# Hybrid decoder layer on eight cores: another arrangement of the last output tiles, and a later slot for the decode masks

## What is computed

```python
h = rmsnorm(x, norm_gain)
q, k, v, g_gla, gk_lr, u, b_gate, c_gate, g_conv = split(h @ w_in)
o, S_new = gla(q, k, v, log_sigmoid(gk_lr @ w_gk_up + b_gk) / 16, S0)   # gated linear attention, 4 heads
o = rmsnorm(o, gla_norm_gain) * silu(g_gla)
yc = b_gate * conv3(c_gate * u) * silu(g_conv)                           # 512 channels
out = x + concat(o, yc) @ w_out
y = rmsnorm(out, final_norm_gain)
```

## Time and profile before

| | |
|---|---|
| median of 3 runs | 315.29 us (314.78 to 315.7) |
| profiled execution | 317.33 us |
| its span on the slowest core (core 1), first to last instruction | 315.8 us |
| spans of the other cores | 311.4 to 314.9 us |
| PE busy | 294.1 us (93%) |
| DVE busy | 236.6 us (75%) |
| ACT busy | 183.9 us (58%) |
| POOL busy | 88.0 us (28%) |

### The profile page before, as it was taken

How to read it: one execution, slowest core, us unless ns; L and a number is a source line. 1 busy time by engine, 2 the same in 40 slices (tenths; PEclk the granted TensorE clock), 3 DMA queues, 4 the chain that set the end, 5 groups by cost and what they waited for, 6 DMA issues and landing times.

```text
span 315.8 us, 6265 instructions; the slowest of 8 cores (311.4 to 315.8 us)
## 1 busy us (share of the span) xinstructions
PE 294.1 (93%) x1870; PEld 147.5 (47%) x1870; DVE 236.6 (75%) x414; ACT 183.9 (58%) x490; POOL 88.0 (28%) x96
## 2 busy tenths in 40 slices
PE   0399999999999979999999999999999999999991
PEld 0284444455444645644444344545444445554460
DVE  3446674979867679999966597899974837889565
ACT  3618535694774538757536668786428536464245
POOL 2995000123233315222332332113306132101050
PEclk9999899999999999999999999989999999999996
DMA  6999999999125032376998743464573311102445
GB/s 162 204 165 163 166 163 170 290 177 202 67 52 185 30 108 95 94 179 144 194 220 243 241 118 113 159 196 35 135 181 136 101 66 66 36 17 66 130 166 208
DMA packets 39873, 44.57 MB, mean 141 GB/s; under 512 B 20952, under 2 KB 29920, under 8 KB 39456
## 3 DMA queue, kind: packets, MB, share of 16 engines
q1 hardware_dynamic: 34800, 32.06, 37.9%
q0 software_dynamic: 4752, 11.77, 21.7%
q10 hardware_dynamic: 288, 0.35, 0.3%
HBM read 38.16 MB, written 10.95 MB: 156 GB/s over the span
## 4 chain that ended last, share of the span: by engine, by line
PE 90%; issue 2%; DVE 2%; DMA 2%; ACT 2%; DVEq 0%; ACTq 0%
PE ps L673 45%; PE ps L683 17%; PE ps L886 8%; PE ps L841 7%; DMA idp_sb<-idp 2%; PE ps L649 2%; PE ps L669 2%; PE ps L1083 2%; PE ps L935 1%; PE ps L797 1%; PE ps L770 1%; PE ps L772 1%; DVE hT L651 1%; PE ps L1238 1%; PE ps L897 1%
## 5 line engine op out<-in xcount | busy, mean ns | idle before, releaser
L673 PE MATMUL ps<-hT,w_in_bf 128*128 128x512 bf16 x656 | 152.6, 385 | 0.2 <-DVE X L692 0.2
L673 PEld LDWEIGHTS ps<-hT,w_in_bf 128*128 128x128 bf16 x656 | 63.7, 99 | 73.3 <-issue 11.0
L703 POOL TENSOR_TENSOR X<-X,fg_sb 128x1024 f32<-128x1024 f32 x14 | 33.9, 2420 | 83.4 <-ACT xs L603 42.9
L660 ACT ACTIVATE f<-ps 128x512 f32<-128x512 f32 (+1 forms) x34 | 19.8, 585 | 39.8 <-PE ps L673 21.4
L603 ACT ACTIVATE xs<-X 128x1024 bf16<-128x1024 f32 x29 | 30.5, 1051 | 20.4 <-DVE X L692 17.5
L683 PE MATMUL ps<-w_out_bf,mixC 128*128 128x512 bf16 (+1 forms) x136 | 35.3, 367 | 0.0
L683 PE MATMUL ps<-w_out_bf,mixG 128*128 128x512 bf16 (+1 forms) x136 | 33.2, 367 | 0.0
L692 DVE TENSOR_TENSOR X<-ps,X 128x512 f32<-128x512 f32 x28 | 19.1, 687 | 18.4 <-PE ps L683 17.8
L886 PE MATMUL ps<-w_v_bf,hT 128*128 128x512 bf16 x128 | 29.5, 379 | 0.0
L841 PE MATMUL ps<-w_in_bf,hT 128*128 128x512 bf16 x96 | 22.7, 379 | 0.0
L661 ACT ACTIVATE f<-f 128x512 f32<-128x512 f32 (+1 forms) x34 | 20.9, 618 | 1.7
(11 more groups left out here) (196 smaller groups left out, 456.2 us busy)
## 6 DMA issues: line engine op xcount, KB each, us to landing
X<-x_all SPq DMA_DIRECT2D x23, 512.0 KB, 5.6
y<-X SPq DMA_DIRECT2D x14, 512.0 KB, 2.9
w_in_bf<-w_in_l POOLq DMA_DIRECT2D x24, 256.0 KB, 21.3
w_out_bf<-w_out_l POOLq DMA_DIRECT2D x2, 1024.0 KB, 51.1
X<-gla_in SPq DMA_DIRECT2D x8, 256.0 KB, 4.7
gla_s<-X SPq DMA_DIRECT2D x8, 256.0 KB, 4.5
w_v_bf<-w_v_l POOLq DMA_DIRECT2D x1, 1024.0 KB, 23.0
X<-x_all POOLq DMA_DIRECT2D x2, 512.0 KB, 37.6
```

Source lines behind the costliest of these rows:

```text
L660: op("act", lambda e: e.activation(out=f.t[:, 0:W], in_=bank.t[:, 0:W], func=AF.Exp, scale=-1.0), dur, [bank.r], [f.r], key, fill)
L673: op("pe", lambda e: [e.matmul(out=bank.t[:], lhsT=w_in_bf[:, c, kc, :], rhs=hT.t[:, kc, :], start=(kc == 0), stop=(kc == KC - 1)) for kc ...
L703: op("pool", lambda e: e.tensor_tensor(out=xb.t[:], in0=xb.t[:], in1=fgb.t[:], op=ALU.mult), 2.4, [xb.r, fgb.r], [xb.r], key + 2, fill)
```

## The change

Four edits:

1. Decode masks: each group's four masks are planned at a cost of 1.6 instead of 1.0 us, and not earlier than 14 planner microseconds before the group's key (112, 124, 136, 148). The instructions are the same.
2. Item 3, tile 1 (`whole`): gain and scaling in one VectorE instruction instead of GpSimd's L703 and a scaling.
3. Item 3, tile 2: Square by halves with a running sum, gain and scaling in two VectorE instructions of 512 columns, each with its store.
4. Item 3, tile 3: one half and two quarters in place of four quarters; the gain of the left half in one GpSimd instruction of 512 columns in place of two VectorE ones of 256. In item 3 the matmuls of the right half of tile 1, and all of tiles 2 and 3, are one operation of 8 instead of 7 and 1. The buffers of tiles 2 and 3 are tracked by half, and by half and quarters.

```diff
-        def out_tile(lhs, parts, m_res, rows, r0, key, fill=False, xb=None, port_free=False, lead=14):
+        def out_tile(lhs, parts, m_res, rows, r0, key, fill=False, xb=None, port_free=False, lead=14, whole=False):
...
+            def half_done(hf, bank):
+                cs = slice(hf * 512, (hf + 1) * 512)
+                op("dve", lambda e: e.tensor_tensor(out=xb.t[:, cs], in0=bank.t[:], in1=xb.t[:, cs], op=ALU.add), 0.69,
+                   [bank.r, xb.R[hf]], [xb.R[hf]], key + hf)
+                op("act", lambda e: e.activation(out=junk2.t[:, cs], in_=xb.t[:, cs], func=AF.Square, accum_out=sums.t[:, hf:hf + 1]), 0.77,
+                   [xb.R[hf]], [junk2.R[hf], sums.R[hf]], key + hf)
+                if hf == 0:
...
+                    return
...
+                for q in range(2):
+                    qs = slice(q * 512, (q + 1) * 512)
+                    op("dve", lambda e, qs=qs: e.scalar_tensor_tensor(out=xb.t[:, qs], in0=xb.t[:, qs], scalar=sums.t[:, 4:5], in1=fgb.t[:, qs],
+                                                                      op0=ALU.mult, op1=ALU.mult), 0.75, [xb.R[q], sums.R[4], fgb.r], [xb.R[q]], key + 2)
+                    dma("sp", lambda e, qs=qs: e.dma_start(out=y_d[r0:r0 + rows, qs], in_=xb.t[0:rows, qs]), _Slot(None, "yt2_%d" % q), [xb.R[q]], [],
+                        key + 3, rows * 2 * KB, out=True)
...
-            if port_free:
+            if whole:
                 op("dve", lambda e: e.scalar_tensor_tensor(out=xb.t[:], in0=xb.t[:], scalar=st.t[:, 2:3], in1=fgb.t[:], op0=ALU.mult, op1=ALU.mult),
                    1.28, [xb.r, st.r, fgb.r], [xb.r], key + 3)
...
         def out_tile_last(lhs, parts, m_res, r0, key, xb):
...
-            for q in range(4):
+            W = [slice(0, 512), slice(512, 1024)]
+            Q = [slice(0, 512), slice(512, 768), slice(768, 1024)]
+            for q in range(3):
                 bank = PS.new()
+                n = Q[q].stop - Q[q].start
+                out_mm(bank, slice(0, 512) if q == 0 else slice(q * 256 - 256, q * 256), 1 if q else 0, lhs, parts[1], m_res, key + 0.1 * q, False)
...
-                if q < 2:
-                    op("dve", lambda e, q=q: e.tensor_tensor(out=pf.t[:, Q[q]], in0=xb.t[:, Q[q]], in1=fgb.t[:, Q[q]], op=ALU.mult), 0.4,
-                       [xb.R[q], fgb.r], [pf.R[q]], key + 0.1 * q)
+                if q == 0:
+                    op("pool", lambda e: e.tensor_tensor(out=pf.t[:, W[0]], in0=xb.t[:, W[0]], in1=fgb.t[:, W[0]], op=ALU.mult),
+                       1.25, [xb.R[0], fgb.r], [pf.r], key)
...
+            if last and t:
+                parts = [parts if t == 1 else [(0, 8, [b.r for b in mc])], [(0, 8, [b.r for b in mc])]]
+            else:
+                parts = [parts, parts]
...
                 op("dve", lambda e, G=G, vmv=vmv: [e.tensor_scalar(out=vmv()[:, s, :], in0=vts.t[:],
                                                                    scalar1=prm_t[:, PO_SEL + 4 * G + s:PO_SEL + 4 * G + s + 1], scalar2=None,
-                                                                   op0=ALU.mult) for s in range(4)], 1.0, [vts.r, prm.r], [vm.r], kg, True)
+                                                                   op0=ALU.mult) for s in range(4)], 1.6, [vts.r, prm.r], [vm.r], kg, True, kg - 14.0)
```

More of the change, by code:

```diff
@@ L685, in out_mm @@
                 op("pe", mm, 0.163 + (hi - lo) * (n / 2400.0 + 0.0025), m_res + res + [B_wout[hf].r], [bank.r], key, fill)
-        def out_tile(lhs, parts, m_res, rows, r0, key, fill=False, xb=None, port_free=False, lead=14):
+        def out_tile(lhs, parts, m_res, rows, r0, key, fill=False, xb=None, port_free=False, lead=14, whole=False):
             xb = xb or x_load(r0, key - lead, key - lead)
+            if port_free:
+                sums = one("sums", [128, 5], F32, 5)
+                junk2 = XS.new(2)
+            def half_done(hf, bank):
[5 more added lines that the diff above has]
+                if hf == 0:
+                    op("act", lambda e: e.activation(out=sums.t[:, 2:3], in_=sums.t[:, 0:1], func=AF.Identity, scale=1.0 / D, bias=EPS),
+                       0.25, [sums.R[0]], [sums.R[2]], key)
+                    return
+                op("act", lambda e: e.activation(out=sums.t[:, 3:4], in_=sums.t[:, 1:2], func=AF.Ln, scale=1.0 / D, bias=sums.t[:, 2:3]), 0.25,
+                   [sums.R[1], sums.R[2]], [sums.R[3]], key + 1)
+                op("act", lambda e: e.activation(out=sums.t[:, 4:5], in_=sums.t[:, 3:4], func=AF.Exp, scale=-0.5), 0.2,
+                   [sums.R[3]], [sums.R[4]], key + 1)
+                for q in range(2):
[4 more added lines that the diff above has]
+                        key + 3, rows * 2 * KB, out=True)
@@ L733, in out_tile_last @@
[L733 to L744, removed]
+            junk = XS.new(3)
@@ new lines, in out_tile_last @@
+            op("act", lambda e: e.activation(out=acc.t[:, 5:6], in_=acc.t[:, 2:3], func=AF.Ln, scale=1.0 / D, bias=acc.t[:, 4:5]), 0.25,
+               [acc.R[2], acc.R[4]], [acc.R[5]], key + 1)
+            op("act", lambda e: e.activation(out=acc.t[:, 6:7], in_=acc.t[:, 5:6], func=AF.Exp, scale=-0.5), 0.2,
+               [acc.R[5]], [acc.R[6]], key + 1)
+            fo = [_Res(), _Res()]
+            op("act", lambda e: e.activation(out=xb.t[:, W[0]], in_=pf.t[:, W[0]], func=AF.Copy, scale=acc.t[:, 6:7]), 0.72,
+               [pf.r, acc.R[6], xb.R[0]], [fo[0]], key + 1)
@@ new lines, in out_tile_last @@
+            op("dve", lambda e: e.scalar_tensor_tensor(out=xb.t[:, W[1]], in0=xb.t[:, W[1]], scalar=acc.t[:, 6:7], in1=fgb.t[:, W[1]],
+                                                       op0=ALU.mult, op1=ALU.mult), 0.75, [acc.R[6], fgb.r] + xb.R, [fo[1]], key + 1)
+            for h, q in enumerate(("act", "sp")):
+                dma(q, lambda e, h=h: e.dma_start(out=y_d[r0:r0 + 128, W[h]], in_=xb.t[:, W[h]]),
+                    _Slot(xb, "yl%d" % h), [fo[h]], [], key + 1, 256 * KB, out=True)
@@ L1026, in item @@
                 hb = HT.new(5)
-                late = [_Part(hb, hb.R[0:1], 0, 1024), _Part(hb, hb.R[1:5], 1024, 2048)]
+                late = [_Part(hb, hb.R[0:2], 0, 1024), _Part(hb, hb.R[2:5], 1024, 2048)]
                 for k, xb in enumerate(late):
@@ L1038, in item @@
                     out_tile(lhs, parts, [m.r], 128, r0 + t * 128, base + 70 + 6 * t + (6 if i == 0 else 0),
-                             xb=kept[t] if i == 0 else late[0] if last and t == 2 else None, port_free=last and t > 1, lead=20 if last else 14)
+                             xb=kept[t] if i == 0 else late[0] if last and t == 2 else None, port_free=last and t > 1, lead=20 if last else 14, whole=last and t == 1)
         def out_sample(key):
```

34 lines of the change are left out of this document (18 added, 16 removed).

## The result

The changed kernel took **312.27 us** (median of 4 runs), the kernel before 315.5 us beside it on the same chip: a ratio of 0.9898 [0.9873, 0.9923], 3.2 us less. The prediction was 312.8 us, inside 311.6 to 315.4, with 0.70 on faster. A repeat on another chip gave 311.89 us and 0.9914 [0.99, 0.9928]. The total came out as forecast. The two terms of the sum did not: the masks gave more than the 1.5 us counted, and the end of the core that sets the time is no shorter than before.

The account below looks back on a forecast made before the run. TensorE's work was taken to bound the kernel, plus 1.9 us of waits and what follows the last matmul. Gains of 1.5 us (masks) and 1.0 us (end), 2.5 us together, gave 312.8 us from 315.29; range 311.6 to 315.4.

Parts of the forecast that it names:

- The wait at L1125: TensorE's 1.7 us wait for kTs at a decode matmul: to shrink by 1.2 to 1.7 us, 1.5 taken.
- (a): Rival: about 1.5 us of TensorE waits come back at other places, only the end gains; 314.3 us, chance 0.18.
- (c): Rival: nothing comes of it, the masks' wait stays and VectorE's loads bound the end; 315.3 us, chance 0.07.
- scan not blocked: Scan L1102 ahead of kTs starts at 107.57, kTs is made by about 109.0; all 1.7 us of wait go.
- scan blocked: GpSimd's multiplication holds scan L1102 until 110.0, kTs is ready at about 111.6; the wait shrinks by 1.2 us.
- Masks in the full stretch: VectorE, 120 to 160: 4.2 us of masks into 1.0 us of air, costed at nothing since state updates may slide.
- Rival (d): Masks moved into VectorE's stretch at 120 to 160 delay results TensorE needs, 5.3 us of waits; 318.1 us, chance 0.11.
- The end: From last matmul to last store issue, 4.05 us: to be 1.0 us shorter, bounds 0.4 and 1.3.
- It just fits: VectorE's 4.3 us of scalings and adds from 304.92 fill the 4.3 us up to the last add's end at 309.25.
- since TensorE waits for no load: Reason given for counting as nothing that later masks hold fewer X buffers over 106 to 135 us.
- Rival (b): Half of tile 2 ahead of the last add waits for GpSimd, so only the masks' change gains; 313.8 us, chance 0.12.

Follow-up runs that it names:

- masks_behind: The kernel before, with only the twelve masks ahead of kTs in VectorE's list moved behind it, cost and times unaltered: 313.85 us, ratio 0.9924.
- masks_cost: The kernel before with the masks' planned cost at 1.6 instead of 1.0, but no earliest time: 313.04 us, ratio 0.9947.
- masks_only: The kernel before with only the masks' change (cost 1.6, not before key - 14), old end kept: 312.81 us, ratio 0.989.
- end_only: The changed kernel with the masks' line as before (cost 1.0, no earliest time): 316.59 us, ratio 1.0 to the kernel before.
- x1_first: The changed kernel with tile 1's load of x issued ahead of tile 2's load in SP's list: 311.49 us, ratio 0.9848 to the kernel before.
- x1_first_b: x1_first run again on a third chip, beside x1_sum_b: 312.59 us, ratio 0.9869 to the kernel before.
- x1_sum: x1_first with the second running sum (L764) ahead of the last Square in ScalarE's list: 311.01 us, ratio 0.9889 to the kernel before.
- x1_sum_b: x1_sum run again on a third chip, beside x1_first_b: 312.89 us, ratio 0.9882 to the kernel before.

## Why the prediction was right, and where only the total was

**The wait at L1125.** Right: it went, no new wait came after 60 us on the slowest core, rivals (a) and (c) didn't come. My middle, 1.5, stood between "scan not blocked", 1.7, and "scan blocked", 1.2. The scan is blocked where it starts under GpSimd's multiplication: 2.47 to 2.48 us on all sixteen cores of masks_behind and masks_cost. In the changed kernel it starts at that multiplication's end and takes 0.48. But the 1.2 was worked out wrongly: with the scan over at 110.4 the prediction still lets ScalarE's L1105 follow "at 110.86 as now", where now the scan ends at 110.76. L1105 starts 0.09 us behind the scan in masks_behind, so kTs would have been made 0.4 us earlier than the 111.6 written, before TensorE comes at 111.16 or with it, and this branch, too, was worth the whole 1.7. All 1.9 us of waits went.

**The size of edit 1.** This is the term of the sum that was mis-sized: 1.5 was forecast, 3.5 measured (masks_only). Of the 3.5, 1.9 are the waits in the list. Up to 1.7 more is the time at 1.2 GHz behind the wait, on those cores that fell to it. The rest is small: counted from start to start of matmuls on cores at full clock, L886, where TensorE stood before L1125, takes 29.77 us in the kernel before and 27.91 in masks_only, L814, ahead of the 0.2 us wait, 2.11 and 1.73, L841 and L897 together 23.69 and 23.33: 2.6 us in all. How often a core falls to the lower clock, the mean clocks of the runs tell: in the trace of end_only the four cores with the drop have 0.984 to 0.988, the others 0.991 to 0.998, and in ten of the twelve runs of end_only the slowest core has 0.984 to 0.986, in 14 of 17 runs of the kernel before beside it 0.983 to 0.985. In masks_only's six runs no core is below 0.988. So the time was nearly always that of a core that had paid both. This is an inference from mean clocks; no run takes the drop away and leaves the wait. That 2.6 + 1.7 is more than the 3.5 measured fits what masks_only lost at its end, 0.8 us on its slowest core (4.87 for 4.07). The account stays rough: die 1 of that chip lost another microsecond at a clock of 0.81 at 28 to 35 in all these kernels, and each core begins its work at its own moment (8.4 to 10.2 us into the span in the kernel before), so the slowest core of one kernel isn't the slowest of the other.

**Masks in the full stretch.** Costed at nothing, and right: 38.76 us busy for 39.01. The cover is the one I named, the state updates' last matmul moved from 167.8 to 184.7, and one more: the last masks slid themselves, to 174. Rival (d) was priced at 318.1; no wait of it came.

**The end.** Forecast 1.0 us. The mechanism was right where the loads were in time: 3.12 for 4.07 us on four cores; the last add starts 0.1 us behind the last matmul and takes 0.42, as worked out, and one running sum is left behind the last Square. The step that failed is "From 304.92 ... 4.3 us, in the 4.3 us to 309.25. It just fits", and with it the reasoning on the loads, that "since TensorE waits for no load" they may be passed over. TensorE doesn't wait for tile 1's x; VectorE does. A plan that fills its 4.3 us to the last tenth has no room for operands 1.7 us late, and tile 1's scaling, now one instruction of 1.28 us on VectorE, stood in front of the last tile's adds. The rows of the kernel before have such a late load as well, core 1, timelines of SP and VectorE:

```profile
295.53 0.33 SPq L597 DMA_DIRECT2D X<-x_all  x1
...
303.11 1.49 DVE L692 TENSOR_TENSOR X<-ps,X 128x512 f32<-128x512 f32 x2 [1.95 <-PE ps L683]
```

It was used 7.6 us after its issue, but issued 13.2 us ahead of the last matmul, and cost that end nothing. With the new times of the masks it is issued only 11.7 us ahead, and the prediction took the end of the old layout for that of the new one. Since the slowest core was one with a late load, its end took 4.15 us for the 4.10 before: no gain. Against masks_only, the old end behind the same issue of loads, the late cores take 3.4 to 4.15 for 4.2 to 4.87, but the times don't show this: 0.989 there, and 0.9898 and 0.9914 for the changed kernel on other chips. With the load first, 4.07 - 3.12 = 0.95 us are gained on every core, and the time on one chip is 312.81 (masks_only) - 311.49 (x1_first) = 1.3 us less; the part of it over 0.95 fits what masks_only lost to its late loads.

end_only leaves a question. In its trace the end is 0.7 us shorter than before on seven cores, and its time is the same as before's, to +-0.6 us. The interval all but refuses the 0.7. The drop of the clock is in both kernels' slowest cores, so it doesn't settle it; where the gain went stays open.

**Rival (b)**, GpSimd's multiplication blocking the end: the two halves of tile 2 (L710) did take 2.10 us for 1.5 under it on core 7, but behind the last add, where I had them, and next to nothing waited for that: the last scaling (L772) starts 0.17 us behind the Exp (L767) on all eight cores. In end_only it did cost something: the first half takes 1.54 to 1.84 us, and L772 starts 0.44 to 0.47 us behind the Exp on all eight cores. That is the 0.3 us between its 3.4 us and the 3.1 of the changed kernel.

So the total was right by luck, two errors against one another: 1.5 + 1.0 was forecast, 3.5 + 0 is what the runs give, measured 3.2. (The chances have a slip besides: "same" adds up to 0.19 and "slower" to 0.11.)

## What to carry to other kernels

Read a wait of the bounding engine on all cores and look at its clock just behind it: the wait's own 1.7 us was about half of what its removal gave here. When a list is packed tight at the end, ask of each operand when its load lands on the worst core, also for loads that the bounding engine never waits for; here the rewritten end gave the slowest core nothing until one load was issued one place earlier. After an edit that lets a planner lay out everything anew, don't reckon with the old moments of the rest: the masks, over 100 us earlier, moved the loads of the end by 1.5 us. And a cost given too low to a planner (1.0 for 1.4) is a defect by itself: correcting that number alone took away 1.3 of the 1.7 us.

## What the hardware showed that was not expected

**The clock after a short wait.** After 1.7 us without a matmul, the granted clock was 0.50 to 0.51 for 3.4 us on two cores of eight (kernel before) and four of eight (end_only), and 1.00 on the others, with the same work on all. After waits of 0.4 us it fell on none of sixteen, and neither after single waits of 1.83, 1.69, 1.48 and 1.41 us at 41 to 43 us (masks_cost core 5, x1_first_b core 2, x1_sum core 1, x1_sum_b core 3). So a wait of this length needn't lead to it. What decides between two cores that ran alike isn't in these traces.

**Loads of the two cores of a pair.** The load of tile 1's x lands late on one core of a neighbouring pair: in the changed kernel 1, 4 and 7 (6.5 to 6.6 us from issue to use), with 2 in between (5.8), in its repeat 1, 2, 5 and 6. Each time it is the core of the pair whose three loads (1.5 MB) are issued later. The DMA view of the changed kernel, 288 to 300 in slices of 0.3 us, GB/s of core 6 and then of core 7:

```profile
GB/s 0 0 0 0 0 0 0 0 27 273 423 437 341 355 287 369 382 382 301 328 287 396 328 191 109 27 27 0 14 0 0 0 0 0 0 0 0 0 0 96
```

```profile
GB/s 123 164 369 382 410 150 68 0 0 0 0 0 0 0 0 0 0 0 0 0 0 191 259 382 396 423 410 410 410 396 410 437 423 437 232 26 27 15 0 0
```

Core 6 issues at 289.73 and moves from 290.4 on; core 7 issues at 291.57 and moves nothing until 294.3, about when core 6 is done. From there it moves about 410 GB/s in nearly every slice. So this is not two cores sharing a rate, it is one going behind the other, if the two spans begin at about the same time, which the trace doesn't say. Cores 0 and 1, in contrast, both drop in places, to 205 to 290 and to 68 to 300, with their loads issued 0.3 us apart. The Trainium skill (HBM Reference, section "Specifications (TRN2)") says that the two cores of a domain share its bandwidth, about 358 GB/s each with both streaming; the slices of cores 0 and 1 are compatible with that, the 2.7 us of standstill on core 7 isn't explained by it.
